# Prompt attention heads and memory blocks of layer 0 run as one sequence, with score banks in turn and page requests during it

## The chip, the cores and the metric

The kernel runs on one core of one Trainium2 chip. The metric is the device time of one execution in microseconds (us); lower is better. A core has a matrix engine (TensorE; PE in the profile, with its weight loads as PEld), a vector engine (VectorE, DVE), an activation engine (ScalarE, ACT), GpSimd (POOL) and a queue engine for DMA requests (SyncE, SP). Each engine works through its own list of instructions in order; semaphores tie the lists together.

## What is computed

The reference is one inference step of a two-layer decoder for a prompt of 1024 tokens and 8 samples of 4 new tokens each. The change lies in the attention of layer 0:

```python
# prompt, 8 heads, blocks of 128 queries, causal
s = _mla_scores(ql, qr, latent, k_rope)          # q.k over latent and rope parts
s = jnp.where(kpos[None, :] <= qpos[:, None], s, -jnp.inf)
p = jax.nn.softmax(s, axis=-1)
o = jnp.einsum('bhqk,bkc->bhqc', p, latent)
# memory cross-attention, 4 heads, 256 memory rows, all queries of prompt and samples
s = jnp.einsum('bthd,bmhd->bhtm', q, mk) * (DH_M ** -0.5)
p = jax.nn.softmax(s, axis=-1)
y = jnp.einsum('bhtm,bmhd->bthd', p, mv)
# samples: softmax over 16 cached pages of 128 rows each (found by a page table) and the new tokens
carry, _ = lax.scan(page_step, init, page_table.T)
```

Each branch is multiplied by SiLU of its gate, the branches are concatenated and go through one output projection. Everything is float32.

## The kernel before, in words

Layer 0 comes first: input projection, recurrence and memory keys and values, then the attention stage at 338 to 599 us, then the attention of the samples over the cached pages up to 699 us, the output projection, and layer 1.

The attention stage before has two parts. The first, `pe_attention`, `act_attention` and `dve_attention`, goes through 64 head units. A unit is one head and one block of 128 queries; its width is the number of keys that the causal mask leaves, 128 to 1024. Units come two heads at a time, and per two heads in the order of blocks 7, 0, 6, 1, 5, 2, 4, 3, both heads for each block, so two wide units are followed by two narrow ones. A unit's path is: TensorE writes scores to PSUM (L893); VectorE adds the mask to the diagonal block (L970), takes the row maximum (L971) and scales it (L972); ScalarE exponentiates (L942); TensorE transposes the probabilities (L905) into one of two banks in turn; ScalarE copies them out (L953); TensorE multiplies values for both heads of a block (L917) and spreads the reciprocals (L922); VectorE multiplies both into `mx` (L983, L984). The scores of unit n lie in banks 0 and 1 for even n and 2 and 3 for odd n, whatever the width, so the scores of n+1 wait until unit n-1 is exponentiated. `between(n)` puts other work between units: for n of 0 to 11, 18 to 26 and 34 to 42 one piece of the projections that make the next heads' queries, keys and values (`piece`, L2833 to L2853; its copy on ScalarE is L2696 to L2704). Each piece waits for the copy of the one before.

The second part, `pe_blocks` and its two partners, goes through eight memory blocks of 128 queries, all four memory heads in one: scores (L1017), maxima (L1100, L1103), four exponentials (L1071), eight transposes (L1028), copies (L1082), values (L1041) and reciprocals (L1048), products (L1112, L1113). The samples' memory attention lies between the blocks (`MS_AT`; on TensorE L1493, L1502, L1511, L1524).

The queues: SP asks for the cached pages (L2531) and POOL for their rotated keys (L2606), 16 requests for each of eight rounds; three rounds have room. Both wait for the last head output before round 0, since most of that room is memory that the heads use. From round 3 on they wait for an earlier round to be used up. SP asks for the value weights `w_uv` (L2526) ahead of round 2, and TensorE waits for them (`tbl_in`) before the samples' attention begins. That attention turns the pages of a round (L1634), makes scores (L1660, L1664) and multiplies values (L1692).

## Time and profile before

| | us |
|---|---|
| median of 3 runs | 1530.68 (1528.85 to 1533.22) |
| the profiled execution's own time | 1530.99 |
| its span in the profile | 1529.4 |
| TensorE busy in the span | 1430.1 |
| head units on TensorE | 337.9 to 554.6 |
| memory blocks on TensorE | 554.6 to 598.1 |

The span is what the hardware profiler covers; the execution's own time is 1.6 us longer. A stretch's busy time is the union of an engine's instructions in it, so length less busy time is idle time. In lists of waits each line says which engine and line waited, for which line of which engine, for how long in total, how often, and the longest. The granted clock is given as a share of TensorE's full speed of 2.4 GHz.

### The profile page before, as it was taken

Reading aid. Unit: us, or ns where it says so; the run is one execution under the profiler, and the core shown is the slowest. Engines: PE = TensorE matmul, PEld = TensorE weight load, DVE = VectorE, ACT = ScalarE, POOL = GpSimd, SP = SyncE. Lnnn points to the kernel's source line nnn. Section 1 sums busy time; section 2 is a strip of 40 time slices with the busy share of each in tenths; the row PEclk is TensorE's granted clock in tenths of the full one; section 3 lists DMA queues with packets and bytes.
Section 4 is the critical chain, followed back from the end, with each engine's and each line's share of the span. In section 5 each row is a group of like instructions: output and inputs, shape, how many; then the busy total and the mean of one; then the engine's idle time right before and its main releaser. Section 6 shows DMA issues by size and latency. Waiting matters only on the chain.

```text
span 1529.4 us, 23928 instructions
## 1 busy us (share of the span) xinstructions
PE 1430.1 (94%) x9592; PEld 1268.6 (83%) x9592; DVE 795.8 (52%) x1471; ACT 571.8 (37%) x1021; POOL 112.1 (7%) x211
## 2 busy tenths in 40 slices
PE   6999999999999878888998999999999999999994
PEld 6988999776566556557997889899999989999994
DVE  4475553164644555554688323323444446745677
ACT  3147421135455555442355133302454104403343
POOL 1000000000000032540000200001000001000000
PEclk9999999999999999999999999999999889999997
DMA  6110132220000033553565320112443202113562
GB/s 205 44 42 28 28 111 68 85 106 13 1 1 32 25 102 100 174 172 125 172 208 202 137 96 29 56 42 61 66 70 56 90 28 98 44 53 128 170 204 101
DMA packets 59488, 136.60 MB, mean 89 GB/s; under 512 B 8985, under 2 KB 37882, under 8 KB 58610
## 3 DMA queue, kind: packets, MB, share of 16 engines
q1 hardware_dynamic: 49298, 113.68, 22.9%
q0 software_dynamic: 10080, 21.39, 6.0%
q8 instruction: 77, 1.26, 0.3%
q14 instruction: 33, 0.27, 0.0%
HBM read 121.53 MB, written 13.50 MB: 88 GB/s over the span
## 4 chain that ended last, share of the span: by engine, by line
PE 83%; DVE 7%; ACT 4%; issue 4%; DMA 1%; POOLq 0%; SPq 0%; POOL 0%; ACTq 0%; DVEq 0%
PE ps L539 15%; PE ps L541 14%; PE ps L540 14%; PE ps L593 4%; PE ps L594 4%; PE ps L595 4%; PE ps L893 3%; PE ps L917 2%; PE ps L1153 2%; PE ps L905 2%; PE ps L1634 2%; DVE stat L971 1%; PE ps L2837 1%; PE ps L2846 1%; PE ps L1660 1%
## 5 line engine op out<-in xcount | busy, mean ns | idle before, releaser
L539 PE MATMUL ps<-x_hi,w_hi 128*128 128x352 f32 x1416 | 472.7, 334 | 15.2 <-DVE w_lo L487 11.4
L541 PE MATMUL ps<-x_hi,w_lo 128*128 128x352 f32 x1416 | 458.4, 324 | 0.0
L540 PE MATMUL ps<-x_lo,w_hi 128*128 128x352 f32 x1416 | 458.0, 323 | 0.0
L539 PEld LDWEIGHTS ps<-x_hi,w_hi 128*128 128x128 f32 x1416 | 269.2, 190 | 25.7 <-issue 12.7
L540 PEld LDWEIGHTS ps<-x_lo,w_hi 128*128 128x128 f32 x1416 | 270.0, 191 | 2.4 <-issue 1.2
L541 PEld LDWEIGHTS ps<-x_hi,w_lo 128*128 128x128 f32 x1416 | 268.6, 190 | 0.0
L481 ACT ACTIVATE w_hi<-w_raw 128x1024 fp32r<-128x1024 f32 (+1 forms) x107 | 123.2, 1152 | 299.0 <-PE ps L541 189.9
L487 DVE TENSOR_TENSOR w_lo<-w_raw,w_hi 128x1024 fp32r<-128x1024 f32 (+1 forms) x107 | 143.5, 1342 | 66.7 <-ACT w_hi L481 66.3
L593 PE MATMUL ps<-mx_hi,w_hi 128*128 128x352 f32 x480 | 158.0, 329 | 1.5 <-DVE mx_lo L683 1.2
L594 PE MATMUL ps<-mx_lo,w_hi 128*128 128x352 f32 x480 | 154.4, 322 | 0.0
L595 PE MATMUL ps<-mx_hi,w_lo 128*128 128x352 f32 x480 | 154.2, 321 | 0.0
L513 DVE COPY z<-ps 128x352 f32<-128x352 f32 x90 | 47.0, 523 | 190.8 <-PE ps L541 190.7
L501 ACT ACTIVATE sig<-ps 128x352 f32<-128x352 f32 x72 | 33.4, 464 | 191.1 <-PE ps L541 191.1
L593 PEld LDWEIGHTS ps<-mx_hi,w_hi 128*128 128x128 f32 x480 | 90.6, 189 | 3.0 <-DVE mx_lo L683 1.3
L594 PEld LDWEIGHTS ps<-mx_lo,w_hi 128*128 128x128 f32 x480 | 90.8, 189 | 0.8
L595 PEld LDWEIGHTS ps<-mx_hi,w_lo 128*128 128x128 f32 x480 | 90.5, 189 | 0.0
L515 DVE TENSOR_TENSOR mx<-sig,ps 128x352 f32<-128x352 f32 x54 | 28.1, 520 | 119.9 <-ACT sig L501 119.7
L2606 POOL DMA_DIRECT2D ropeT<-in_cache_rope x128 | 63.6, 496 | 285.6 <-issue 239.2
L942 ACT ACTIVATE probs<-ps,stat 128x1024 f32<-128x1024 f32 (+7 forms) x64 | 47.4, 741 | 98.2 <-DVE stat L972 97.8
L893 PE MATMUL ps<-kT,qT 96*128 96x512 f32 (+4 forms) x192 | 75.5, 503 | 0.5 <-ACT qs L2704 0.5
L905 PEld LDWEIGHTS ps<-ident,probs 128*128 128x128 f32 x288 | 32.8, 141 | 35.8 <-ACT probs L942 25.9
L905 PE MATMUL ps<-ident,probs 128*128 128x128 f32 x288 | 43.2, 277 | 16.5 <-ACT probsT L953 8.5
(453 smaller groups left out, 1853.9 us busy)
## 6 DMA issues: line engine op xcount, KB each, us to landing
w_raw<-in_w_out SPq DMA_DIRECT2D x48, 640.0 KB, 3.9
w_raw<-in_w_in SPq DMA_DIRECT2D x59, 512.0 KB, 3.6
page<-in_cache_mla SPq DMA_DIRECT2D x128, 128.0 KB, 2.7
kvs<-in_mem_cache SPq DMA_DIRECT2D x16, 512.0 KB, 5.5
x_res<-in_xT SPq DMA_DIRECT2D x24, 176.0 KB, 2.3
x<-x_next POOLq DMA_DIRECT2D x3, 1408.0 KB, 7.2
x_res<-x SPq DMA_DIRECT2D x24, 176.0 KB, 2.4
w_mem<-in_w_mem SPq DMA_DIRECT2D x2, 2048.0 KB, 9.6
```

The costliest lines, as they stand in the source:

```text
L481: act.activation(w_hi[:, u % 2, 0:n], w_raw[:, u % 2, 0:n], ACT.Copy).then_inc(w_hi_ready, 1)
L487: dve.tensor_tensor(w_lo[:, u % 2, 0:n], w_raw[:, u % 2, 0:n], w_hi[:, u % 2, 0:n], ALU.subtract).then_inc(w_split, 1)
L539: pe.matmul(out, w_hi[:, u % 2, kk], x_hi[:, k, chunk(c)], start=(k == 0), stop=False)
L540: pe.matmul(out, w_hi[:, u % 2, kk], x_lo[:, k, chunk(c)], start=False, stop=False)
L541: mm = pe.matmul(out, w_lo[:, u % 2, kk], x_hi[:, k, chunk(c)], start=False, stop=(k == KX - 1))
L593: pe.matmul(out, w_hi[:, u % 2, kk], mx_hi[:, k, chunk(c)], start=(k == 0), stop=False)
L594: pe.matmul(out, w_hi[:, u % 2, kk], mx_lo[:, k, chunk(c)], start=False, stop=False)
L595: mm = pe.matmul(out, w_lo[:, u % 2, kk], mx_hi[:, k, chunk(c)], start=False, stop=(k == KM - 1))
L893: mm = pe.matmul(s[:, a:b], q_of(u), k_of(u, a, b), start=True, stop=True)
L905: mm = pe.transpose(ps[:, 4 + f % 2, (kt - k0) * P:(kt - k0 + 1) * P], pr[:, kt * P:(kt + 1) * P], ident[:, :])
L942: act.activation(probs_of(n, u), scores_of(n, u), ACT.Exp, bias=stat[:, n % 4:n % 4 + 1], scale=MLA_SCALE, accum_out=stat[:, 4 + n % 4:5 + ...
L2606: gp.dma_start(ropeT[32 * j:32 * j + 32, r % 3, q * P:q * P + P], x["cache_rope"][bass.ds(four[q], 1), :, :].rearrange("a c p -> (a c) p") ...
```

## The change

The memory blocks become units of the same sequence. It now has 72 units: memory blocks 0, 1, 2 and 3 stand behind the first four head units (blocks 7 and 0) of each two heads, block 4 behind the next four units of the last two heads, and blocks 5, 6 and 7 at the end. Narrow units, up to 512 keys, now take one score bank, wide ones and memory blocks take two, from four banks in turn; `ISSUE` says after which units the scores of others are written, up to two units ahead. Every output, of heads or of a memory block, is one of 40 parts that use bank 6 in turn. The steps of the samples' memory attention move to head units 50 to 59. SP asks for the pages of round 0 as soon as the samples' memory values are made, then for `w_uv`, and for rounds 1 and 2 after the last head output; POOL asks for rounds 0 and 1 as soon as the projection pieces are done and for round 2 after the last head output. The buffers of round 0's pages and of rounds 0 and 1's rotated keys lie in other memory than before, which is free earlier. TensorE waits for `w_uv` where it uses it. Later counts of the memory semaphores lose layer 0's share.

The core of the diff. First the sequence, then TensorE's part of it:

```diff
-        Unit = namedtuple("Unit", "h q nk m")
+        Unit = namedtuple("Unit", "h q nk bank after")
+        Part = namedtuple("Part", "p q nk first second")
+
+        def order_of_units():
+
+            for p in range(H // 2):
+                for a in range(NT // 2):
+                    for q in (NT - 1 - a, a):
+                        for r in range(2):
+                            yield 2 * p + r, q
+                    if a == 0 or (p, a) == (3, 1):
+                        yield None, p + a
+            for b in range(5, NT):
+                yield None, b
+        UNITS, PARTS, PART_OF, HEAD_UNIT, pos, owner = [], [], [], [], 0, [-1] * 4
+        for n, (h, q) in enumerate(order_of_units()):
+            nk = T if h is None else (q + 1) * P
+            width = (nk + 511) // 512
+            UNITS.append(Unit(h, q, nk, pos % 4, max(owner[b % 4] for b in range(pos, pos + width))))
+            for b in range(pos, pos + width):
+                owner[b % 4] = n
+            pos += width
+            if h is None or h % 2 == 0:
+                PARTS.append(Part(None if h is None else h // 2, q, nk // P, n, n if h is None else n + 1))
+            PART_OF.append(len(PARTS) - 1)
+            HEAD_UNIT.append(None if h is None else sum(u.h is not None for u in UNITS) - 1)
+        ISSUE = {n: [] for n in range(-1, len(UNITS))}
+        for n, u in enumerate(UNITS):
+            ISSUE[max(u.after + 1, n - 2) if n else -1].append(n)
+        assert all(n in ISSUE[-1] + ISSUE[n - 1] + ISSUE.get(n - 2, []) for n in range(1, len(UNITS)))
+        LAST_HEAD_PART = max(g for g, w in enumerate(PARTS) if w.p is not None)
...
             def scores(n):
                 u = UNITS[n]
-                if n >= 2:
-                    pe.wait_ge(p_ready, n - 1)
+                if u.after >= 0:
+                    pe.wait_ge(p_ready, u.after + 1)
+                if u.h is None:
+                    for h in range(HM):
+                        r = (h % 2) * 64
+                        mm = pe.matmul(head_scores(u, h), z[r:r + 64, Z_QM + h // 2, u.q * P:u.q * P + P],
+                                       kmT[r:r + 64, h // 2, :], start=True, stop=True)
+                    mm.then_inc(sc_ready, 1)
+                    return
...
-            def output(m):
-                w = PAIRS[m]
+            def output(g):
+                w = PARTS[g]
                 pe.wait_ge(pt_ev, FILLS[w.second][1])
+                if g:
+                    pe.wait_ge(o_done, g)
+                if w.p is None:
...
             scores(0)
             for n in range(len(UNITS)):
-                if n + 1 < len(UNITS):
-                    scores(n + 1)
-                between(n)
+                for k in ISSUE[n]:
+                    scores(k)
+                if HEAD_UNIT[n] is not None:
+                    between(HEAD_UNIT[n])
                 transposes(n)
-                if pair_at(n) is not None:
-                    output(pair_at(n))
-            output(len(PAIRS) - 1)
+                if part_done_at(n) is not None:
+                    output(part_done_at(n))
+            output(len(PARTS) - 1)
...
@@ -957,7 +1020,8 @@
             for n in range(len(UNITS)):
                 if n + 1 < len(UNITS):
                     exps(n + 1)
-                between(n)
+                if HEAD_UNIT[n] is not None:
+                    between(HEAD_UNIT[n])
                 evacuate(n)
...
+                if u.h is None:
+                    top = mst[:, u.q % 2, M_TOP, :]
+                    for r in range(2):
+                        v.mark(dve.tensor_reduce(top.rearrange("p (t r) -> p t r", r=2)[:, :, r],
+                                                 bank(u.bank + r).rearrange("p (t n) -> p t n", t=2), AX_X, ALU.max))
+                    v.settle()
+                    dve.tensor_scalar(mst[:, u.q % 2, M_NEG, :], top, -MEM_SCALE, None, ALU.mult).then_inc(mx_ready, 1)
+                    return
```

VectorE's `maxima` are called in the order of `ISSUE` as well, then `invert(n)`, `into_mx` of a finished part, and `between`. The removed `pe_blocks`, `act_blocks` and `dve_blocks` held the same arithmetic for memory blocks with the waits `ma_z`, `ma_m`, `ma_p`, `ma_t`, `ma_te`, `ma_o` and `ma_done`. Then the fillers and queues:

```diff
-        MS_AT = dict(scores=2, maxima=4, exps=6, normalise=9, turn=11, evacuate=13, values=15, copy=17, back=19, output=22)
+        MS_AT = {name: 50 + n for n, name in enumerate(
+            ("scores", "maxima", "exps", "normalise", "turn", "evacuate", "values", "copy", "back", "output"))}
 
...
         def dve_between(dve, v, n):
-            if n == MS_AT["maxima"]:
+            if n == 46:
+                dve_qbd(dve, v, 0)
+            elif n == MS_AT["maxima"]:
...
+                if g == 0:
+                    pe.wait_ge(tbl_in, 48)
...
-            pe.wait_ge(tbl_in, 48)
...
-            sp.wait_ge(o_ready, len(PAIRS))
...
-                if r == 2:
+                if r == 0:
                     sp.wait_ge(ms_o, 1)
-                    sp.dma_start(w_uv[:, :, :, :], x["w_uv"]).then_inc(tbl_in, 16)
+                elif r == 1:
+                    sp.wait_ge(o_ready, LAST_HEAD_PART + 1)
...
+                if r == 0:
+                    sp.dma_start(w_uv[:, :, :, :], x["w_uv"]).then_inc(tbl_in, 16)
...
-            gp.wait_ge(o_ready, len(PAIRS))
+            gp.wait_ge(prep_z, N_PIECES)
             for r in range(8):
-                if r >= 3:
+                if r == 2:
+                    gp.wait_ge(o_ready, LAST_HEAD_PART + 1)
+                elif r >= 3:
                     gp.wait_ge(ss_o, 5 * ((r - 3) // 4) + 2 + (r - 3) % 4)
...
-            act_attention(act, lambda n: prep_at(n) and evacuate_piece(prep_at(n)))
-            act_blocks(act, 0, lambda n: act_between(act, n))
+            act_attention(act, lambda n: evacuate_piece(prep_at(n)) if prep_at(n) else act_between(act, n))
```

TensorE's list at the narrow units of block 2 of the last two heads, before. L893 is a unit's scores, L905 its transposes, L917 and L922 an output; the number at the end is how many elements a partition of the result has.

```order
L893 MATMUL ps<-kT,qT 128x384 [waits prep_ev,rope_ready,p_ready]
L905 MATMUL ps<-ident,probs 128x128 [waits pt_ev,p_ready]
...
L917 MATMUL ps<-probsT,vh 64x128 [waits o_done,prep_ev,pt_ev]
...
L893 MATMUL ps<-kT,qT 128x512 [waits prep_ev,rope_ready,p_ready]
L893 MATMUL ps<-kT,qT 128x128
L905 MATMUL ps<-ident,probs 128x128 [waits pt_ev,p_ready]
...
L893 MATMUL ps<-kT,qT 128x512 [waits prep_ev,rope_ready,p_ready]
L893 MATMUL ps<-kT,qT 128x128
L905 MATMUL ps<-ident,probs 128x128 [waits pt_ev,p_ready]
```

The same place now; L930 is scores, L942 transposes, L971 and L976 an output, L1472 a step of the samples' memory attention.

```order
L930 MATMUL ps<-kT,qT 128x384 [waits prep_ev,rope_ready,p_ready] x2
L942 MATMUL ps<-ident,probs 128x128 [waits pt_ev,p_ready]
...
L930 MATMUL ps<-kT,qT 128x512 [waits prep_ev,rope_ready,p_ready]
L930 MATMUL ps<-kT,qT 128x128
L1472 MATMUL ps<-ident,mo_133 128x128 [waits ms_oc]
...
L942 MATMUL ps<-ident,probs 128x128 [waits pt_ev,p_ready]
...
L971 MATMUL ps<-probsT,vh 64x128 [waits prep_ev,o_done,pt_ev]
...
L942 MATMUL ps<-ident,probs 128x128 [waits pt_ev,p_ready]
...
L930 MATMUL ps<-kT,qT 128x512 [waits prep_ev,rope_ready,p_ready]
L930 MATMUL ps<-kT,qT 128x128
```

Before, the scores of the next wide unit were written behind the output of the last one, with one narrow transpose and one score step up to their own transposes. Now they are written two steps earlier, with both narrow transposes, an output and the other wide unit's scores behind them.

TensorE's list where the heads ended and the memory blocks began, before:

```order
L917 MATMUL ps<-probsT,vh 64x128 [waits o_done,prep_ev,pt_ev]
...
L922 MATMUL ps<-ident,stat 64x128 [waits pn_ready]
...
L1017 MATMUL ps<-kmT,z 128x256 [waits p_ready]
L1017 MATMUL ps<-kmT,z 128x256 x7
L1028 MATMUL ps<-ident,probs 128x128 [waits ma_p]
```

And now, around the last heads' outputs, with the scores of memory blocks 5 and 6 (L921):

```order
L921 MATMUL ps<-kmT,z 128x256 [waits p_ready]
L921 MATMUL ps<-kmT,z 128x256 x3
L942 MATMUL ps<-ident,probs 128x128 [waits pt_ev,p_ready]
...
L971 MATMUL ps<-probsT,vh 64x128 [waits prep_ev,o_done,pt_ev]
...
L976 MATMUL ps<-ident,stat 64x128 [waits pn_ready]
...
L942 MATMUL ps<-ident,probs 128x128 [waits pt_ev,p_ready]
...
L921 MATMUL ps<-kmT,z 128x256 [waits p_ready]
```

The scores of the first two memory blocks had nothing behind them but their own transposes; now each memory block's scores have head work or another block's work behind them.

## Rows read from the trace of the kernel before

**Rows 1.** Busy time and idle time by stretch; the columns are named in its first line.

```profile
core 0: us, PE busy (x) PEld busy (x) DVE busy (x) ACT busy (x) POOL busy (x), PEclk, DMA share, GB/s
337.90:503.00 165.10, 153.94 (x1052) 103.84 (x1052) 85.08 (x249) 86.92 (x209) 0.00 (x0) 1.00 0.06 19
503.00:554.60 51.60, 41.80 (x350) 28.25 (x350) 26.27 (x86) 24.72 (x63) 0.00 (x0) 1.00 0.01 2
554.60:598.60 44.00, 35.36 (x396) 26.49 (x394) 23.65 (x71) 25.55 (x87) 23.84 (x48) 0.96 0.60 175
598.60:606.00 7.40, 5.94 (x57) 5.55 (x57) 3.92 (x12) 2.71 (x7) 0.00 (x0) 0.77 0.00 0
```

**Rows 2.** TensorE's waits from 337.9 to 503 us: total, times, longest.

```profile
PE ps L905 <- ACT probs L942: 3.8, 4, 1.0
PE ps L905 <- ACT probsT L953: 3.1, 3, 1.5
PE ps L2837 <- ACT qT L2700: 2.4, 3, 1.0
...
```

**Rows 3.** TensorE's waits from 503 to 554.6 us.

```profile
PE ps L905 <- ACT probsT L953: 5.4, 5, 1.3
PE ps L905 <- ACT probs L942: 4.2, 4, 1.2
PE ps L917 <- ACT probsT L953: 0.7, 1, 0.7
```

**Rows 4.** TensorE's waits from 554.6 to 600 us, the last memory blocks' end among them.

```profile
PE ps L1028 <- ACT probs L1071: 3.7, 1, 3.7
PE ps L1028 <- ACT probsT L1082: 3.4, 3, 1.5
PE ps L1041 <- DVE mx L1113: 1.1, 1, 1.1
```

**Rows 5.** Timeline of wide head units: start, duration, instruction, idle time before it.

```profile
518.20 1.77 PE L893 MATMUL ps<-kT,qT 96*128 96x512 f32 x4
...
519.92 1.67 PE L893 MATMUL ps<-kT,qT 128*128 128x512 f32 x4
...
521.66 1.01 ACT L942 ACTIVATE probs<-ps,stat 128x896 f32<-128x896 f32 x1 [5.11 <-DVE stat L972]
...
522.81 0.98 PE L905 MATMUL ps<-ident,probs 128*128 128x128 f32 x7 [1.22 <-ACT probs L942]
```

**Rows 6.** TensorE's timeline of memory blocks.

```profile
560.26 1.97 PE L1028 MATMUL ps<-ident,probs 128*128 128x128 f32 x8 [3.69 <-ACT probs L1071]
...
592.64 1.06 PE L1028 MATMUL ps<-ident,probs 128*128 128x128 f32 x8 [1.32 <-ACT probsT L1082]
593.63 1.09 PE L1041 MATMUL ps<-probsT,vm 128*64 128x128 f32 x16
594.56 0.61 PE L1048 MATMUL ps<-ident,mst 128*64 128x128 f32 x8
596.23 1.09 PE L1041 MATMUL ps<-probsT,vm 128*64 128x128 f32 x16 [1.07 <-DVE mx L1113]
```

**Rows 7.** VectorE's and ScalarE's timeline of one memory block.

```profile
588.55 1.28 DVE L1100 TENSOR_REDUCE mst<-ps 128x2 f32<-128x512 f32 x2
...
590.08 0.47 ACT L1071 ACTIVATE probs<-ps,mst 128x256 f32<-128x256 f32 x1 [0.93 <-DVE mst L1103]
...
591.89 1.09 ACT L1082 ACTIVATE probsT<-ps 128x512 f32<-128x512 f32 x2
```

**Rows 8.** Timeline of SP's page requests, then of TensorE's first use of rounds 1 and 2.

```profile
556.38 19.18 SPq L2531 DMA_DIRECT2D page<-in_cache_mla  x32
...
609.84 1.53 PE L1634 MATMUL ps<-ident,page 128*128 128x128 f32 x12
...
620.40 4.04 PE L1634 MATMUL ps<-ident,page 128*128 128x128 f32 x32
```

**Rows 9.** The page requests' time from issue to landing.

```profile
DMA to landing us min/median/max: 1.9/2.7/5.1
```

More of the change, by code:

```diff
@@ L840, in k_of, with part_done_at, scores_of, head_scores @@
             return kT[rows_of_head(u.h), u.h % 4, a:b]
-        UNITS = [Unit(2 * p + r, q, (q + 1) * P, 8 * p + 2 * a + w)
-                 for p in range(H // 2) for a in range(NT // 2) for w, q in enumerate((NT - 1 - a, a))
-                 for r in range(2)]
-        Pair = namedtuple("Pair", "p q nk first second")
-        PAIRS = [Pair(u.h // 2, u.q, u.nk // P, n, n + 1) for n, u in enumerate(UNITS) if n % 2 == 0]
-        assert [UNITS[w.first].m for w in PAIRS] == list(range(32))
-        def pair_at(n):
-            return n // 2 - 1 if n % 2 == 0 and n else None
-        def scores_of(n, u):
-            return flat(ps[:, 2 * (n % 2):2 * (n % 2) + 2, :])[:, 0:u.nk]
+        def part_done_at(n):
+            return PART_OF[n - 1] if n and PARTS[PART_OF[n - 1]].second == n - 1 else None
+        def scores_of(u):
+            return flat(ps[:, u.bank:u.bank + 2, :])[:, 0:u.nk] if u.nk > 512 else ps[:, u.bank, 0:u.nk]
+        def head_scores(u, h):
+            return ps[:, u.bank + h % 2, NMEM * (h // 2):NMEM * (h // 2) + NMEM]
         def probs_of(n, u):
@@ new lines, in into_mx @@
+            def into_mx(g):
+                w = PARTS[g]
+                dve.wait_ge(o_ready, g + 1)
+                if w.p is None:
+                    out = mx[:, 8:10, w.q * P:w.q * P + P]
+                    value, rec = (ps[:, 6, a:a + 2 * P].rearrange("p (t n) -> p t n", t=2) for a in (0, 2 * P))
+                else:
+                    out = mx[:, w.p, w.q * P:w.q * P + P]
+                    value, rec = ps[:, 6, 0:P], ps[:, 6, P:2 * P]
+                v.then(dve.tensor_tensor(out, out, value, ALU.mult))
+                dve.tensor_tensor(out, out, rec, ALU.mult).then_inc(o_done, 1)
@@ L986, in dve_attention @@
             maxima(0)
             for n in range(len(UNITS)):
-                if n + 1 < len(UNITS):
-                    maxima(n + 1)
+                for k in ISSUE[n]:
+                    maxima(k)
                 invert(n)
-                if pair_at(n) is not None:
-                    into_mx(pair_at(n))
-                between(n)
-            into_mx(len(PAIRS) - 1)
-        M_NEG, M_SUM, M_REC, M_TOP = range(4)
-        def block_probs(b):
-            return probs[:, b % 2, :].rearrange("p (h n) -> p h n", h=HM)
@@ L1131, in prep_at @@
+                if part_done_at(n) is not None:
+                    into_mx(part_done_at(n))
+                if HEAD_UNIT[n] is not None:
+                    between(HEAD_UNIT[n])
+            into_mx(len(PARTS) - 1)
         def prep_at(n):
@@ L2788, in rope_at @@
                     rope_sum(6 + n - 34)
+                else:
+                    dve_between(dve, v, n)
             for step in range(3):
```

202 lines of the change are left out of this document (56 added, 146 removed).

## The prediction

> **What bounds the kernel now.** I read the page first: TensorE is busy most of the span, so time can only come from its idle time, from its work, or from its clock. Its work doesn't change (the same 72 units and the same samples' steps), so I cut the attention stage into stretches by busy time [rows 1]. From 337.9 to 503 us TensorE is idle for 165.10 - 153.94 = 11.2 us, from 503 to 554.6 for 51.60 - 41.80 = 9.8, and in the memory blocks from 554.6 to 598.6 for 44.00 - 35.36 = 8.6. That is 29.6 us of idle time in 260.7. VectorE and ScalarE are each busy for only some 135 us of these 260.7, so neither can become the bound by its total. The stage after it begins only when this one is through, and nothing else is waited for there: a microsecond of idle time saved is one of the kernel's, as far as the samples' stage doesn't wait for something new.
>
> Then I asked who TensorE waits for. Up to 503 us it waits 3.8 + 3.1 = 6.9 us in 7 gaps at the transposes L905 [rows 2]; the other 4.3 of its 11.2 are mostly waits of projection pieces for the copy of the piece before, 2.4 of them at L2837. From 503 on, where no pieces lie between the units, it waits 5.4 + 4.2 + 0.7 = 10.3 us in 10 gaps [rows 3], the first of which begins before 503. In the memory blocks it waits 3.7 us once for the first block's exponentials, 3.4 in three gaps for copies out of the transposes' banks, and 1.1 for the last product but one [rows 4]. The gaps are chains of latency. The reader can follow one [rows 5]: scores written from 518.20 to 519.97; mask, maximum and scaling until the exponential starts at 521.66; transposes at 522.81. From the end of the scores to the transposes are 2.84 us, and TensorE has only a narrow unit's transpose and one other score step of 1.67 us (the row at 519.92) for them; 1.22 us stay open.
>
> **The change at the head units.** The scores of a wide unit are now written two steps ahead: behind them lie two narrow units' transposes, the wide output and the other wide unit's scores. Even for the narrowest such pair in the stretch this is over 4 us of TensorE's work against a chain of 2.8. At narrow units both scores stand ahead of the second wide transposes, and the next wide scores between these and the narrow transposes, so the copy of the first bank has a wide score step's time, 1.67 in [rows 5] for 896 keys, where it had a narrow one's. Walking through VectorE's and ScalarE's new lists with the durations of the trace, I find neither late at a head unit, but margins of only 0.2 to 0.8 us in several places. So of the 6.9 + 10.3 = 17.2 us I let a fifth stand, 3.5, and count 13.7 as saved. The bounds: all of it saved, or half of it (8.6), since half of the gaps are waits for ScalarE's copies, which keep their place in its list. The 4.3 us at pieces and at the start stay: a piece still waits for the copy of the piece before, and ScalarE still makes this copy between an exponential and a copy of transposes.
>
> **The memory blocks.** A block asks VectorE and ScalarE for a chain of 590.08 - 588.55 = 1.53 us from maxima to exponentials and 591.89 - 590.08 = 1.81 for the four of them, then 1.09 for the copies [rows 7]; 3.3 us from scores to transposes. Blocks 0 to 4 now have two or more transposes, an output and a wide score step of head units behind their scores, 4.2 us or more without pieces, so these cost no new gap; the 3.7 us at the first block go. At the end three blocks still follow each other. There I walk as follows. Block 5 is covered by head work. Block 6's transposes come after block 5's, the last heads' output and block 7's scores, some 5 us behind its own scores: no gap. Block 7 has only block 6's transposes and block 5's output behind its scores, 1.06 + 1.6 = 2.7 (the output is 593.63 to 595.17) against 3.3: 0.6 open, and as much again for the second bank's copy. The last output waits for the product of the one before, 1.07, as at 596.23 [rows 6]. Together 2.3; I take 2.5, with 4.5 (all of rows 4 but the first gap) as the upper bound and 1.1, the last product's wait alone, as the lower one. Of 8.2 this saves 5.7. The samples' memory steps take the same TensorE work between other units; their partners on VectorE and ScalarE lie one head unit apart, which is over 2 us each, so I cost them at nothing; behind them are the units' own transposes, and if a step came late, one of 1 us would be lost for each of three steps, which the upper bound of the head gaps takes in.
>
> **The clock.** The gap of 3.7 us is followed by eight transposes in 1.97 us where others take 1.06 [rows 6]: TensorE ran at the lower of its two levels, 1.2 GHz, for a while. The granted clock over these 44 us is 0.96 [rows 1], so 44 x 0.04 = 1.8 us went. With the gap this goes too; between gaps of up to 1.5 us in the stretches before the clock stayed at 1.00. I take 1.6, bounds 0 and 1.8. The low clock of 0.77 from 598.6 on stays: the wait ahead of it, for VectorE's copies at the start of the samples' stage, is the same.
>
> **The requests.** Round 0 is asked for at head unit 56, some 30 us before the stage's end, and 16 requests take 19.18 / 32 x 16 = 9.6 us [rows 8], so it is there. Round 1 now starts only behind the last head output. From there to the end of the stage are block 6's and 7's transposes, block 7's scores and three outputs, 2 x 1.06 + 1.1 + 3 x 1.6 plus the gaps of 2.3 = 10.3 us, and its first use comes 609.84 - 598.6 = 11.2 later: 21.5 us against 9.6 + 5.1 for the slowest landing [rows 9] = 14.7. Round 2 has 10.3 + 620.40 - 598.6 = 32.1 against 24.3. POOL asks for round 2's rotated keys in the same time. Margins of 6.8 and 7.8 us hide all of it. Rounds 3 to 7 wait for the samples' own progress, as before. `w_uv` is asked for before round 1 and used only behind the first half's last values: nothing. Its wait at the first scores of the samples goes, but these waited for VectorE.
>
> **The sum.** Saved: 13.7 at the head units, 5.7 at the memory blocks and 1.6 of clock: 21.0 us. Against the profiled execution's own 1530.99 (its span of 1529.4 and 1.6 around it; the median of the runs, 1530.68, is within 0.3 of it) this gives **1510.0 us**. Bounds: 17.2 + 7.1 + 1.8 = 26.1 saved gives 1504.9; 8.6 + 3.7 + 0 = 12.3 gives 1518.7.
>
> **A rule against it.** TensorE idled in 10 gaps of up to 1.3 us between 503 and 554.6 while its two pairs of score banks took turns, and was granted 1.00 throughout [rows 1, 3]. The Trainium skill ("TensorE: Matmul & The Clock Gate", "A second HAM failure mode: psum-queue depth-cycling") says that a kernel which cycled through PSUM banks in every iteration left TensorE idle so often between groups of matmuls that its clock swung between half and full. By that rule the new turn of banks would cost clock; the trace of before, which has shorter work between longer gaps, doesn't agree.
>
> **Rivals.**
> *The head gaps stay.* If the chain were set by ScalarE's list, not by when scores are written, the 17.2 us would remain and the change would save 5.7 + 1.6 = 7.3: **1523.7**. For it: most gaps name ScalarE. Against: before many of its exponentials it is idle itself for VectorE, 5.11 us in [rows 5].
> *Memory blocks cost gaps in the middle.* The four exponentials of 1.81 us stand ahead of the copies of the unit before. If that opened a gap as long for each of blocks 0 to 4, 9.1 us would come back: **1519.1**. Against: 4.2 us or more of cover.
> *A page round comes late.* If page requests took twice as long between other traffic, round 1 would need 24.3 us for its 21.5 and round 2 some 43 for its 32: 11 us lost, **1521**. Against: DMA is at 0.60 share in the old place and less in the new.
> *Slower: the output bank becomes the pace.* All 40 outputs use bank 6 and wait for the product of the part before, and VectorE now reads finished parts behind more maxima. If each of 39 waited the 1.07 us seen once [rows 6], 41.7 us would be added: **1551.7**. It turns slower by over 4.6 us from a mean wait of (21.0 + 4.6) / 39 = 0.66 us. Against: no head output waited for it before.
> *Slower: the clock.* If the stage's 229 us of work were granted 0.77 as after 598.6 [rows 1], 229 x (1 / 0.77 - 1) = 68 us come on top: **1578**. It turns slower below a granted clock of 0.90.
>
> **How the numbers follow.** The forecast has 0.74, the head gaps 0.10, gaps in the middle 0.05, a late round 0.04, the output bank 0.04, the clock 0.03. A measurement here can tell some 0.3% (4.6 us) from no change. The forecast and the next three are faster, but the head gaps' case, with a few further microseconds lost, can end within 0.3%: I put 0.04 of it there. So faster 0.89, same 0.04, slower 0.07. The range is 1504 to 1521: the forecast's bounds, widened to take in the gaps in the middle and a late round; outside stay the head gaps and the slower cases, 0.17.
>
> **What would show it.** Right: TensorE's idle time over the stage near 10 us (4.3 + 3.5 + 2.5), no gap over 1.5 us in it but at its very end, granted clock 1.00 in all of it, its end near 577 us, and from there to the first output projection the same 100 us as before. Wrong: waits of TensorE for ScalarE at head transposes above 5 us in all; a wait for a page or a rotated key at round 1 or 2; waits for the product in `mx` at many outputs; a granted clock below 0.97 inside the stage.

## The result and the profile after

The changed kernel takes **1503.85 us** (median of 5 runs, 1500.38 to 1505.93), the kernel before 1528.85 (median of 5 runs, with the three shown above among them). The two medians lie 25.0 us apart. The ratio, taken over all runs, is 0.9828, with a 95% interval of 0.9814 to 0.9842; of 1528.85 us that is 26.3 saved, 24 to 28. The forecast of 1510.0 saved 21.0 of the 1530.99 it started from; the measured time lies 0.15 us below the lower end of its range, 1504.

The profiled execution of the changed kernel took 1500.38 us for itself, with a span of 1498.8; it was the shortest of the five. Its page begins with the busy time of each engine (share of the span, instructions):

```profile
span 1498.8 us, 23935 instructions
PE 1419.3 (95%) x9592; PEld 1263.2 (84%) x9592; DVE 793.8 (53%) x1471; ACT 572.3 (38%) x1021; POOL 112.5 (8%) x211
```

The attention stage runs from its first head scores to the first scores of the samples. By stretch, columns as in [rows 1], first the stage of the kernel before as one:

```profile
337.91:599.92 262.01, 231.10 (x1795) 158.61 (x1796) 136.09 (x409) 137.17 (x357) 23.84 (x48) 0.99 0.14 42
```

and of the kernel after as one, then the beginning of the samples' stage:

```profile
337.36:572.68 235.32, 225.95 (x1795) 159.09 (x1796) 134.14 (x409) 137.30 (x357) 23.92 (x48) 1.00 0.13 39
572.68:580.00 7.32, 6.60 (x65) 5.78 (x69) 3.38 (x8) 3.85 (x8) 0.00 (x0) 0.77 0.81 239
```

The stage went from 262.0 to 235.3 us. That is 26.7 us less with the same number of matmul instructions, and of it 30.9 - 9.4 = 21.5 are idle time of TensorE and 231.10 - 225.95 = 5.15 are *busy* time. The other 3.9 of the 30.6 us between the two profiled executions lie in the samples' stage (100.3 to 98.7), in all that follows (829.2 to 827.5) and ahead of the stage (0.5); executions of one and the same kernel differ by as much there, as the table below shows.

What TensorE still waits for in the stage (us in all, times, longest) is short enough to be shown whole but for the wait at its very end:

```profile
PE ps L942 <- ACT probsT L1016: 5.5, 8, 1.0
PE ps L956 <- DVE mx L1065: 1.1, 1, 1.1
PE ps L2792 <- ACT qT L2656: 0.8, 1, 0.8
PE ps L930 <- ACT qs L2660: 0.5, 1, 0.5
```

Transposes L942 are L905 and L1028 of the kernel before, exponentials L1005 are L942 and those of L1071 are L1000. Waits for exponentials, eight gaps at head units and 3.7 us at the first block [rows 2 to 4], are gone altogether; what stays are mostly waits for copies out of the transposes' banks. The last row's wait lies just ahead of the stage's first scores, before and after, and is in no count of gaps below.

Here is the place where the scores of a wide unit moved: block 4 of the last two heads. First the kernel before (start, duration, instruction, in brackets the idle time ahead of it):

```profile
540.72 1.35 PE L893 MATMUL ps<-kT,qT 96*128 96x512 f32 x4
541.90 0.49 PE L905 MATMUL ps<-ident,probs 128*128 128x128 f32 x3
542.24 1.25 PE L893 MATMUL ps<-kT,qT 128*128 128x512 f32 x4
544.43 0.76 PE L905 MATMUL ps<-ident,probs 128*128 128x128 f32 x5 [0.95 <-ACT probs L942]
```

Then the kernel after:

```profile
543.24 1.25 PE L930 MATMUL ps<-kT,qT 96*128 96x512 f32 x4
...
545.05 0.52 PE L942 MATMUL ps<-ident,probs 128*128 128x128 f32 x3
545.50 1.53 PE L971 MATMUL ps<-probsT,vh 128*64 128x128 f32 x24
...
547.18 0.55 PE L942 MATMUL ps<-ident,probs 128*128 128x128 f32 x3
547.56 1.25 PE L930 MATMUL ps<-kT,qT 128*128 128x512 f32 x4
548.64 0.71 PE L942 MATMUL ps<-ident,probs 128*128 128x128 f32 x5
```

The scores of 543.24 are those of 540.72 before, and the transposes of 548.64 those of 544.43. Between them now lie both narrow units' transposes, an output, the other wide scores and a step of the samples' memory attention, 5.40 us from start to start where it was 3.71, and no gap is left. Only the first of two wide units moves so. Where a memory block stands behind the narrow units, as behind blocks 7 and 0, it is the block whose scores go two ahead, and the wide unit after it keeps its place, one ahead. This is so at the very units of [rows 5]:

```profile
518.36 1.67 PE L930 MATMUL ps<-kT,qT 96*128 96x512 f32 x4
519.87 1.04 PE L942 MATMUL ps<-ident,probs 128*128 128x128 f32 x8
...
523.45 0.95 PE L942 MATMUL ps<-ident,probs 128*128 128x128 f32 x7 [0.25 <-ACT probsT L1016]
```

Here the memory block's eight transposes (519.87) and an output stand between, and of the gap of 1.22 us a wait of 0.25 for a copy is left. And the end of the stage, answering to [rows 6], with the instruction that had to wait in the last row:

```profile
562.01 1.07 PE L942 MATMUL ps<-ident,probs 128*128 128x128 f32 x8 [0.81 <-ACT probsT L1016]
...
565.35 1.07 PE L942 MATMUL ps<-ident,probs 128*128 128x128 f32 x8 [0.82 <-ACT probsT L1016]
...
568.95 1.09 PE L956 MATMUL ps<-probsT,vm 128*64 128x128 f32 x16 [1.07 <-DVE mx L1065]
...
572.68 0.33 PE L1599 MATMUL ps<-z,qs 128*32 128x32 f32 x16 [1.87 <-DVE stat L1738]
```

Eight transposes of a memory block take 1.04 to 1.07 us in these rows; those of the first block took 1.97 before [rows 6]. The requests, answering to [rows 8]: SP's round 0, the value weights and the start of round 1,

```profile
539.23 8.69 SPq L2483 DMA_DIRECT2D page<-in_cache_mla  x16
547.95 0.43 SPq L2487 DMA_DIRECT2D w_uv<-in_w_uv  x1
560.32 40.81 SPq L2483 DMA_DIRECT2D page<-in_cache_mla  x45
```

and TensorE's first uses of rounds 0, 1 and 2:

```profile
573.13 5.38 PE L1585 MATMUL ps<-ident,page 128*128 128x128 f32 x32
582.60 1.53 PE L1585 MATMUL ps<-ident,page 128*128 128x128 f32 x12
...
593.17 4.04 PE L1585 MATMUL ps<-ident,page 128*128 128x128 f32 x32
```

None of the three waits for a transfer.

### The profile page after: what moved, and what is told of

It is laid out like the page before. It is cut to its first block, busy times and chain, and to the rows that moved or that the text cites. A ratio compares the mean times of both kernels' runs of the same rounds, so it can differ in the third digit from the quotient of the medians.

```text
span 1498.8 us, 23935 instructions
## 1 busy us (share of the span) xinstructions
PE 1419.3 (95%) x9592; PEld 1263.2 (84%) x9592; DVE 793.8 (53%) x1471; ACT 572.3 (38%) x1021; POOL 112.5 (8%) x211
## 3 DMA queue, kind: packets, MB, share of 16 engines
q1 hardware_dynamic: 49298, 113.68, 23.5%
## 4 chain that ended last, share of the span: by engine, by line
PE 86%; DVE 6%; issue 3%; ACT 3%; DMA 1%; SPq 1%; POOLq 0%; POOL 0%; ACTq 0%; DVEq 0%
PE ps L543 15%; PE ps L544 15%; PE ps L545 15%; PE ps L597 4%; PE ps L598 4%; PE ps L599 4%; PE ps L930 4%; PE ps L942 2%; PE ps L971 2%; PE ps L1101 2%; PE ps L2792 1%; PE ps L1585 1%; PE ps L2801 1%; PE ps L2796 1%; DMA x_raw<-in_xT 1%
## 5 line engine op out<-in xcount | busy, mean ns | idle before, releaser
L930 PE MATMUL ps<-kT,qT 96*128 96x512 f32 (+4 forms) x192 | 71.9, 497 | 0.5 <-ACT qs L2660 0.5
L1005 ACT ACTIVATE probs<-ps,stat 128x1024 f32<-128x1024 f32 (+7 forms) x64 | 47.6, 744 | 57.8 <-DVE stat L1044 57.8
L942 PEld LDWEIGHTS ps<-ident,probs 128*128 128x128 f32 x352 | 40.2, 141 | 23.9 <-issue 12.1
L942 PE MATMUL ps<-ident,probs 128*128 128x128 f32 x352 | 51.5, 276 | 5.6 <-ACT probsT L1016 5.5
```

The costliest lines, as they stand in the source:

```text
L930: mm = pe.matmul(s[:, a:b], q_of(u), k_of(u, a, b), start=True, stop=True)
L942: mm = pe.transpose(ps[:, 4 + f % 2, (kt - k0) * P:(kt - k0 + 1) * P], pr[:, kt * P:(kt + 1) * P], ident[:, :])
L1005: act.activation(probs_of(n, u), scores_of(u), ACT.Exp, bias=stat[:, n % 4:n % 4 + 1], scale=MLA_SCALE, accum_out=stat[:, 4 + n % 4:5 + n ...
```

## The experiments

Each ran beside the kernel before on the same chip: the first four below on one chip, the next four on another, the last four on a third, where the kernel before had medians of 1529.22, 1529.97 and 1530.23 us. The diffs are against the changed kernel. The stage, TensorE's busy time in it, its gaps (the number of waits of TensorE that the view of waits lists in it, without the one at its very end), the samples' stage up to the first output projection and the rest come from the profiled execution of each:

```
                  median   ratio [95%]             stage  busy    gaps  samples  rest
before            1528.85  -                       262.0  231.10  27    100.3    829.2
after             1503.85  0.9828 [0.9814,0.9842]  235.3  225.95  10     98.7    827.5
c0_after          1503.43  0.9833 [0.9815,0.9850]  235.4  225.95  10    101.0    830.6
x1_blocks_end     1503.68  0.9834 [0.9818,0.9851]  237.4  224.92  11     99.2    827.9
x2_old_banks      1531.24  1.0010 [0.9994,1.0027]  264.3  234.82  26     99.5    829.4
x5_one_ahead      1532.73  1.0028 [1.0014,1.0042]  266.1  236.49  26    101.8    827.4
x3_late_requests  1504.49  0.9833 [0.9816,0.9851]  235.4  225.95  10    101.1    831.2
x4_uv_wait_first  1502.52  0.9825 [0.9805,0.9844]  235.3  225.95  10     97.0    829.1
v4_rope4          1499.30  0.9803 [0.9786,0.9820]  235.3  225.94  10     97.2    829.1
v5_rope4_mem5     1502.33  0.9823 [0.9805,0.9840]  236.2  226.01  11     96.6    831.1
x9_wide_early     1507.27  0.9861 [0.9840,0.9881]  238.5  226.29  13    101.7    827.4
x10_narrow_early  1534.19  1.0025 [1.0014,1.0037]  262.8  231.83  27     99.4    830.1
v4_rope4_again    1500.96  0.9819 [0.9800,0.9838]  235.3  225.95  10     96.6    829.5
c0_after_again    1503.71  0.9830 [0.9812,0.9847]  235.3  225.95  10     97.7    828.2
```

Busy time of the stage repeats within 0.01 us from chip to chip, and its length within 0.1. The two other columns of time vary by some 3 us for one kernel (after, c0_after and c0_after_again).

**c0_after: the changed kernel again.**

> The changed kernel once more, as the yardstick for the other three. Measured here: the attention stage, from the first head scores to the first scores of the samples' attention, took 262.0 us before and 235.3 now, of which TensorE was busy 231.1 and 226.0. Theory D (a gap costs more than its idle time: TensorE's pipeline drains before it and fills after it, which the trace books as busy, some 0.2 us per gap): the stage repeats within 0.5 us, busy within 0.5, at 1502 to 1505 us in all. Rival L (the 3.6 us of busy time beyond the clock's share were chance): busy time moves by 2 us or more between two profiles of the same kernel.

1503.43 us, stage 235.4, busy 225.95. The 5.15 us of busy time are no chance of one execution.

**x1_blocks_end: all eight memory blocks behind the heads**, with the new banks and the early scores.

```
-                    if a == 0 or (p, a) == (3, 1):
-                        yield None, p + a
-            for b in range(5, NT):
+            for b in range(NT):
```

> New score banks and scores up to two units ahead, but all eight memory blocks behind the 64 head units. Theory A (it is the early scores that close the head gaps, and head work that closes the blocks' gaps): head gaps as in the change, under 4 us in all; between the blocks five more gaps of 0.8 us with 0.2 of drain each, so the stage takes 240 to 241 us and the kernel 1508 to 1510. Rival B (memory blocks between the heads are what hides the heads' latency too): head gaps of 10 us or more, stage above 248, kernel above 1516. For the projection pieces: if the waits for their copies (from some 4.3 us down to 1.3) went because scores come earlier, they stay near 1.3 here; if they went because memory units lie between them, they are back at 3 to 4.

1503.68 us, the same as after; the stage is 237.4 long, 2 us more. In it TensorE waits 8.6 us in 9 gaps for copies out of the transposes' banks, where after has 5.5 in 8. Of its gaps 5.0 us lie at head units, one of 1.9 among them, against 3.9 in after, and 4.7 at the blocks against 2.7. So the merging itself, the part that the forecast gave 5.7 us to, is worth 2 us of the stage where scores are written early, and nothing that the total shows. In that condition lies the reason: with the first block's scores written ahead of the last heads' transposes and output, its 3.7 us go without any merging. My expectation for this stage, 240 to 241, was too long, and that for the head gaps, under 4 us, too low. The wait at a projection piece stays at the 0.8 us of after.

**x2_old_banks: banks by parity and scores one unit ahead**, with the memory blocks merged as in the change.

```
-            UNITS.append(Unit(h, q, nk, pos % 4, max(owner[b % 4] for b in range(pos, pos + width))))
+            UNITS.append(Unit(h, q, nk, 2 * (n % 2), n - 2 if n >= 2 else -1))
-            ISSUE[max(u.after + 1, n - 2) if n else -1].append(n)
+            ISSUE[n - 1].append(n)
```

> Memory blocks as units between the heads as in the change, but each unit's scores in the old banks (0 and 1 or 2 and 3 by parity) and written one unit ahead. Theory A: the head gaps stay, some 15 to 17 us plus 0.2 us of drain for each, and only the first block's 3.7 us, the clock's 1.8 and part of the blocks' gaps go: stage 252 to 255, kernel 1520 to 1523. Rival B: head gaps mostly gone, stage under 242, kernel under 1510. Theory D: TensorE's busy time in the stage is near 229.3 (only the clock's share gone); rival L has no number for it but none that goes with the number of gaps.

1531.24 us: no gain left at all, where I expected the merging to keep its own. TensorE's waits:

```profile
PE ps L942 <- ACT probsT L1016: 10.3, 11, 1.7
PE ps L942 <- ACT probs L1000: 7.7, 5, 1.9
PE ps L942 <- ACT probs L1005: 5.8, 6, 1.1
```

The second row is the rival of gaps in the middle: five memory blocks each wait 1.0 to 1.9 us for their exponentials, since only one narrow unit's transposes, the next scores and at most a projection piece lie behind their own scores, and together they cost 4 us more than the 3.7 of the first block that they save. Two of the three longest of these waits, and one of the short ones, are followed by a low clock. Three windows around each of the last two show it (columns as in [rows 1], the clock is the third number from the end):

```profile
553.00:556.00 3.00, 1.10 (x7) 0.63 (x5) 2.12 (x7) 2.46 (x10) 0.00 (x0) 0.98 0.00 0
556.00:559.00 3.00, 3.00 (x19) 2.05 (x18) 0.07 (x1) 2.10 (x5) 0.00 (x0) 0.50 0.00 0
559.00:562.00 3.00, 3.00 (x32) 1.64 (x36) 1.82 (x5) 0.00 (x0) 0.00 (x0) 0.95 0.00 0
...
584.00:587.00 3.00, 1.09 (x10) 0.67 (x7) 2.24 (x7) 2.39 (x10) 0.00 (x0) 0.93 0.00 0
587.00:590.00 3.00, 3.00 (x22) 2.67 (x22) 0.00 (x0) 2.83 (x11) 0.00 (x0) 0.50 0.00 0
590.00:593.00 3.00, 3.00 (x34) 2.29 (x32) 1.91 (x5) 0.00 (x0) 1.33 (x3) 1.00 0.38 88
```

TensorE worked 1.10 and 1.09 us out of 3, then all of the next 3 at 1.2 GHz, half of its full clock. The third long wait, 1.80 us ahead of 539.25, has no low clock behind it; in x5 below the same wait has one.

**x5_one_ahead: the new turn of banks, scores one unit ahead.**

```
-            ISSUE[max(u.after + 1, n - 2) if n else -1].append(n)
+            ISSUE[n - 1].append(n)
```

> The change with its new turn of the four score banks, but every unit's scores written one unit ahead. Before, the wait for the bank was long over when scores were reached, so theory A says that the banks alone bring nothing: stage 252 to 255, kernel 1520 to 1523, as with the old banks. Rival C (a free bank lets scores start earlier, how far ahead they stand in the list matters little): stage under 242, kernel under 1510.

1532.73 us, slower than before by 0.28% [0.14, 0.42], with the very waits of x2, to the tenth. So the banks in turn give nothing by themselves. By the program they are the permit for early scores, since a unit's scores may go ahead only into banks that are free; no run had early scores in the old banks. The line moves VectorE's maxima together with the scores, here and in x9 and x10, so what is tested is both. Against x2 the stage is 1.8 us longer, 1.7 of it busy time: the clock was low in four spells of the stage, 13.6 us in all, against three and 10.2 in x2.

**x3_late_requests: round 0 of pages and rotated keys asked for behind the last head output.**

```
                 if r == 0:
                     sp.wait_ge(ms_o, 1)
-                elif r == 1:
                     sp.wait_ge(o_ready, LAST_HEAD_PART + 1)
...
-                if r == 2:
+                if r == 0:
                     gp.wait_ge(o_ready, LAST_HEAD_PART + 1)
```

> The change, but both queues ask for round 0 only behind the last head output, as before the change. That output's product is through some 12 us before the stage ends, round 0's first pages are used 1 us behind the end and its rotated keys 8 us behind it. SP needs 9.6 us for 16 pages and up to 5.1 for landing, POOL 10.6 for 16 requests. Theory P (the early requests only matter if the stage behind would wait): round 0's pages come 1 to 2 us late, rounds 1 and 2 at about the time of use, so 2 to 4 us of waits for DMA ahead of the third round, kernel 1505 to 1508. Rival Q (the early requests are worth nothing): no such wait, 1503.5 as the change. Rival Q2: over 8 us lost, since all three rounds queue one behind the other.

1504.49 us, within the noise of after. TensorE doesn't wait at rounds 0 to 2 even so; its only waits for DMA after the stage are

```profile
PE ps L1611 <- DMA ropeT<-in_cache_rope: 3.0, 1, 3.0
PE ps L1585 <- DMA page<-in_cache_mla: 0.8, 1, 0.8
```

of which the first, at round 7, is in after too. Asking earlier is worth nothing measurable here; the loss that I expected from asking late didn't come.

**x4_uv_wait_first: the wait for the value weights back ahead of the samples' first scores.**

```
-                if g == 0:
-                    pe.wait_ge(tbl_in, 48)
...
+            pe.wait_ge(tbl_in, 48)
             scores(0)
```

> The change, but TensorE waits for the value weights ahead of the samples' first scores, as before the change. They are asked for 24 us before that and TensorE waits there for VectorE anyway (1.9 us). All theories: no difference, within 1 us of the change's 1503.5. If it costs more, landing of this 1 MB transfer takes over 24 us.

1502.52 us: no difference. In after the weights are asked for at 547.95, and the scores wait for VectorE until 572.68 in any case. (The transfer is 512 KB by the profile, and not the 1 MB of my expectation.)

**v4_rope4: a fourth buffer of rotated keys**, so that POOL may ask one round further ahead; an attempt at a faster version.

```
-        ropeT = [ropeT0, ropeT1, ropeT2]
+        ropeT = [ropeT0, ropeT1, ropeT2, ropeT3]
...
-                elif r >= 3:
-                    gp.wait_ge(ss_o, 5 * ((r - 3) // 4) + 2 + (r - 3) % 4)
+                elif r >= 4:
+                    gp.wait_ge(ss_o, 2 + r - 4)
```

> The change with four buffers of rotated keys instead of three, so POOL asks for round 7 one round earlier. In both profiles of the change TensorE waits for the rotated keys of round 7 (3.3 us in the first). Theory K (POOL's requests for round 7 start too late because the buffer is still in use): this wait goes, samples' stage 97 to 98 us instead of 98.7 to 101.0, kernel 1500 to 1502. Rival: the wait is the transfer's own slowness, and it stays or moves to the pages of round 7, whose wait of 0.9 us grows: no gain.

1499.30 us [ratio 0.9786 to 0.9820], the lowest median of all. In after, POOL could ask for the last round only when a buffer came free, and TensorE waited 3.3 us for its round 7:

```profile
640.47 2.23 POOL L2562 DMA_DIRECT2D ropeT<-in_cache_rope  x4 [3.28 <-PE ps L1643]
...
657.78 1.92 PE L1611 MATMUL ps<-latT,qs 128*32 128x512 f32 x16 [3.34 <-DMA ropeT<-in_cache_rope]
```

With the fourth buffer no wait for rotated keys is left, and 0.8 us for pages.

**v5_rope4_mem5: v4, and memory block 5 ahead of the last four head units.**

```
-                    if a == 0 or (p, a) == (3, 1):
+                    if a == 0 or (p, a) in ((3, 1), (3, 2)):
                         yield None, p + a
-            for b in range(5, NT):
+            for b in range(6, NT):
```

> As the kernel with four buffers of rotated keys, and memory block 5 stands ahead of the last four head units instead of behind them, so only blocks 6 and 7 follow each other. Theory A: one of the end's gaps of 0.8 us and its drain go, the rounds behind the last head output keep a margin of some 3 us: stage 234 to 235, kernel 1499 to 1501. Rival: rounds 1 and 2 come late by more than that gives, samples' stage up by 2 us or more.

1502.33 us, stage 236.2: 0.9 longer, with one wait of 1.9 us for a copy of transposes. A miss; the end of the stage isn't mended so.

**x9_wide_early: two ahead only for units of more than 512 keys**, that is wide head units and memory blocks. Of these only the first of two can go early, behind both narrow units' scores.

```
-            ISSUE[max(u.after + 1, n - 2) if n else -1].append(n)
+            ISSUE[max(u.after + 1, n - 2) if n and u.nk > 512 else n - 1].append(n)
```

> The change, but narrow units' scores are written one unit ahead as before; only the first wide unit (or memory block) behind two narrow ones is written two ahead. Theory E (one move makes the whole gain: these wide scores now stand between the last wide transposes and the first narrow ones, and long ahead of their own): both kinds of head gaps stay closed, stage 235 to 238 us, kernel 1503 to 1507. Rival F (the second narrow unit's early scores matter as much): half of the gain of 26.7 us in the stage is lost, stage about 249. Theory D (0.2 us booked as busy per gap): busy time 226 to 227 if the gaps stay some 11 in number.

1507.27 us, stage 238.5. Against x5, from which it differs by this one move, the stage is 266.1 - 238.5 = 27.6 us shorter. Of these, 6.8 are the low clock, which x5 had for 13.6 us and x9 has nowhere; the other 20.8 are gaps and what goes with them. Against before, x9 keeps 23.5 of the change's 26.7. Its waits, the first three rows:

```profile
PE ps L942 <- ACT probsT L1016: 8.2, 11, 1.2
PE ps L956 <- DVE mx L1065: 1.1, 1, 1.1
PE ps L2792 <- ACT qT L2656: 1.0, 1, 1.0
```

Of these 8.2 us, 0.8 + 0.8 are at the last two blocks, so 6.6 are at head units, against 3.9 in after.

**x10_narrow_early: two ahead only for units of up to 512 keys**, the counterpart (the same line with `u.nk <= 512`).

> The converse: only the second narrow unit of two is written two ahead, wide units and memory blocks one ahead. Theory E: all gaps are open as in the kernel with everything one unit ahead (stage 266.1), those at the first narrow transposes even longer, since the narrow scores of 0.4 to 0.8 us no longer stand in front of them: stage 264 to 272, kernel 1530 to 1538. Rival F: half of the gain, stage about 249. Theory D: busy time 235 us or more with 25 to 28 gaps.

1534.19 us, stage 262.8. Its waits for exponentials are those of x5 to the tenth, and its waits for copies are nearly so:

```profile
PE ps L942 <- ACT probsT L1016: 10.2, 9, 2.0
PE ps L942 <- ACT probs L1000: 7.7, 5, 1.9
PE ps L942 <- ACT probs L1005: 5.8, 6, 1.1
```

The stage is 3.3 us shorter than in x5, but the clock explains more than that: it was low in one spell of 3.4 us, which cost 1.7 where x5 lost 6.8. Without the clock's share this stage is 1.8 us longer. So alone the move gives nothing; beside the wide units' early scores it gives 238.5 - 235.3 = 3.2 us. The clock also shows that a gap does not settle it. Here, as in x2, a memory block waits 1.90 us, and TensorE works 1.10 us out of 3:

```profile
550.00:553.00 3.00, 1.10 (x5) 0.46 (x4) 2.44 (x8) 2.14 (x9) 0.00 (x0) 1.00 0.00 0
553.00:556.00 3.00, 2.89 (x23) 1.84 (x23) 0.57 (x3) 2.42 (x6) 0.00 (x0) 1.00 0.00 0
```

The granted clock stayed at 1.00.

**v4_rope4_again and c0_after_again: both once more, on a third chip.**

> The kernel with four buffers of rotated keys once more, beside the change on one chip. Theory K: faster than the change by 2 to 4 us in the medians; samples' stage without a wait for rotated keys. Rival: the 1499.3 us of its first run was chance, both within 1 us.

> The change as the yardstick beside it: 1502 to 1505 us, stage 235.3, samples' stage 98.5 to 101 with 2 to 3.5 us of wait for the rotated keys of round 7.

1500.96 and 1503.71 us, 2.7 apart. On the second chip v4 was 1499.30 beside 1504.49 and 1502.52 of kernels with the same stage as after. The intervals of the ratios overlap each time, the sign is the same both times. That v4 beats the changed kernel, by some 2 to 3 us, is likely and not settled. What TensorE waits for rotated keys and pages in the samples' stage varies between profiles of kernels alike in it: 3.3 + 1.2 us in after, 2.5 + 0.5 in c0_after, 1.4 + 2.3 in c0_after_again; in v4 0 + 0.8 and 0 + 0.6. It may be that this is all of the gain; why the page waits vary, no run tells.

## Why the prediction was right in kind and short in size

Two steps failed, and both made the saving too small: the waits at the projection pieces were kept in the sum and went, and the clock's term was taken for all that busy time could give. The stage lost 26.7 us where the sum had 21.0. That the time then fell just below the range, and not just inside it, is chance: 1530.99 - 26.7 is 1504.3, and the changed kernel's three medians were 1503.4 to 1503.9, while the kernel before had medians of 1528.9 to 1530.2.

**The head gaps: right.** The forecast left 3.5 us of 17.2; 3.9 were left (5.5 of the waits' row less 0.81 and 0.82 at the end). The sign of being wrong, above 5 us of waits at head transposes, did not come. The mechanism was the one told: x10, where the wide unit's scores stay one ahead, keeps the gaps, x9, where they alone go early, loses most. So the rival by which the gaps belong to ScalarE's list fell: in x5 and x2 the list's waits came back with the order of scores. The prediction tells it of any wide unit, and it holds for the first of two; behind a memory block it is the block's scores that go ahead. What the sum had as one move are two unequal ones: counted from x5, the early scores of wide units and memory blocks bring 27.6 us of the stage, 6.8 of them clock, and then the narrow ones' 3.2.

**The memory blocks: 2.7 us left, forecast 2.5, partly by chance.** Of the two copies forecast late at block 7, 0.6 each, one came late, by 0.82; block 6, for which I saw no gap, waited 0.81; the last product's 1.07 came as read. And the cause was misplaced: the forecast put the gain at the merging. x1 shows that blocks all at the end lose only 2 us more, and x2 that merged blocks with scores one ahead lose 4 us more than they save. The rival of gaps in the middle was thus right about the chain (3.3 us, of which one narrow unit's transposes and the next scores don't cover enough), and wrong only in that the scores stand two ahead in the change.

**The pieces' waits: the first step that failed.** "The 4.3 us at pieces and at the start stay": 0.8 stayed. Of the 4.3, the waits at pieces were 3.5, in five gaps; about 0.5 had been counted in [rows 3] as well, whose first gap begins before 503 us (its waits are 10.3 us, the idle time from 503 on is 9.8); the rest is too short to be listed. So 3.5 - 0.8 = 2.7 us went that the sum kept. The argument looked at the wait's releaser, ScalarE's copy, and not at what lies between a piece and the piece before. The runs show that either half of the change takes most of it: x1, with early scores and no block between heads, has 0.8 left, x2 and x5, with blocks between heads and scores one ahead, 1.0 + 0.5, the second at L2808. x9 has 1.0, x10 2.3.

**The clock: the second step that failed.** Its term was 1.6 us, and TensorE's busy time shrank by 5.15. The clock was 1.00 in the whole stage after, as forecast; the one low spell before lasted 3.4 us and cost half of that, 1.7. The remaining 3.45 us the forecast had nowhere: it took a gap to cost its idle time and no more. The rows show that it costs more. The scores at 542.24 before, with a gap behind them, are booked as busy for 1.25 us. The same scores at 547.56 after hold 1.25 too, but the next instruction starts after 548.64 - 547.56 = 1.08. So 0.17 us that overlap with the next instruction where there is one stand alone ahead of a gap, as theory D in the expectation of c0_after has it. Over the whole stage, here is the busy time less what the low clock cost (half of its low spells: 1.7 us before, 5.1 in x2, 6.8 in x5, 1.7 in x10):

```
kernels with 26 or 27 gaps:  before 229.4   x2 229.7   x5 229.7   x10 230.1
kernels with 10 to 13 gaps:  after 225.95   x1 224.9   x9 226.3
```

Two groups, some 4 us apart over some 15 gaps: an estimate of 0.2 to 0.3 us for each gap. That fewer gaps went with less busy time is shown. That it is the gaps and nothing else is not: in all kernels of the second row the wide scores are written early too, and inside a row the number of gaps doesn't order the times, x1 has one gap more than after and 1.0 us less busy time. No run changed the gaps and left the order of TensorE's list alone.

**The sum anew**: 13.3 at head units, 5.4 at blocks, 2.7 at pieces, 0.1 of other idle time, 1.7 of clock and 3.45 of busy time beside it give 26.65, against the stage's 26.7. Without the two surprises, 2.7 and 3.45, it is 20.5, near the forecast's 21.0.

**The clock rule against the change: it did not show.** With the banks in turn the granted clock was 1.00 over 235 us. The Trainium skill's rule ("TensorE: Matmul & The Clock Gate", "A second HAM failure mode: psum-queue depth-cycling") ties the loss to frequent idle spells between groups; in that sense x2 and x5 agree with it, with parity banks and with banks in turn alike: where the blocks' gaps came back, so did spells at half clock, 10.2 and 13.6 us. The turn of the banks by itself is not what costs clock here: with it the stage ran at 1.00 in after, x1 and x9. Nor does a gap always cost it, as x10 shows.

**Requests, output bank, value weights: right.** No wait for a transfer at rounds 0 to 2, none for the product in `mx` but at the stage's last output, so neither the late round nor the output bank became a cost; x3 and x4 show that the parts of the change that move requests and the wait for `w_uv` are worth nothing in either direction. The clock of 0.77 behind the stage and the samples' 100 us (98.7) stayed, as forecast. The stage ended at 572.7 and not near 577, by the two failed steps.

**The range** ended at 1504 because its lower bound was made of the terms' own bounds: all 17.2 and all but 1.1 of the 8.2. None of these reached to a cost left out of the sum, the 2.7 us of pieces and the 3.5 of busy time. So "17.2 + 7.1 + 1.8 = 26.1 saved" was a bound on the terms and none on the stage, which gave 26.7.

## What to carry to other kernels

Where an engine works through its list in order and waits for a chain on others, look for the one place at which a producer's instruction can go one unit earlier, behind what already stands there, and make the buffers permit it; the buffers alone (x5) and the interleaving of other work alone (x2) brought nothing, and on top of both a single move (x9) brought nearly all. When gaps of TensorE are to be closed, expect somewhat more than their idle time: in this kernel an estimated 0.2 to 0.3 us more for each. And set the lower end of a range by all the idle time of the stage, not by the waits that one has an argument for.

## What the runs showed that was not expected

- TensorE's busy time for the same instructions, the low clock's share taken off, differs by some 4 us in 230 between kernels with many gaps and with few: 229.4 to 230.1 us with 26 or 27, 224.9 to 226.3 with 10 to 13.
- Two kernels whose waits agree to a tenth of a microsecond (x2 and x5) differ in how long the clock was low, 10.2 and 13.6 us of the stage. Two gaps of 1.9 us in x2 were followed by 3 us at 0.50, which costs another 1.5 us; a gap of 1.90 us in x10, with as little work around it, was not.
- Asking for round 0 of the pages 21 us later (x3) made no difference to the time, while one more buffer for rotated keys took a wait of 1.4 to 3.3 us away at round 7, which no step of the forecast had looked at.
